# Opening of a two-block diffusion transformer kernel: first modulation tasks as rows on TensorE, token products in a first wave of four banks, token norm beside the QK products

## The reference

```python
def ada_chunks(cvec, w, b):
    m = jax.nn.silu(cvec) @ w + b
    return jnp.split(m[..., None, :], 6, axis=-1)

def modulate(x, g, shift, scale):
    return rms_norm(x, g) * (1 + scale) + shift

def chunk_gmlp(u, v, w_s, b_s, g_v):
    u = jax.nn.gelu(u)
    v = layer_norm(jax.nn.gelu(v), g_v)
    v = v.reshape(bn, length // A_CHUNK, A_CHUNK, A_GROUPS, A_GDIM)
    s = jnp.einsum('gij,bnjgc->bnigc', w_s, v) + b_s.T[None, None, :, :, None]
    return u * s.reshape(bn, length, A_WIDTH)

# layer 0
sh_m, sc_m, ... = ada_chunks(c, w_ada[0], b_ada[0])          # and for c_ctx
xm, cm = modulate(h, g, sh_m, sc_m), modulate(hc, g, csh_m, csc_m)
u, va, q, k, vb = split(t @ w_in)                            # t = xm and cm
y_a, y_b = chunk_gmlp(u, va, ...), neighbourhood_attention(q, k, vb, ...)
```

## Time and profile before

| | us |
|---|---|
| median of 3 runs (4460.9 to 4467.37) | 4466.56 |
| profiled execution, its own time | 4457.49 |
| its span | 4455.7 |
| PE busy | 3872.9 (87%) |
| DVE busy | 2122.0 (48%) |
| ACT busy | 1449.3 (33%) |
| POOL busy | 1549.5 (35%) |

### The profile page before, as it was taken

How to read it: one execution, slowest core, us unless ns; L and a number is a source line. 1 busy time by engine, 2 the same in 40 slices (tenths; PEclk the granted TensorE clock), 3 DMA queues, 4 the chain that set the end, 5 groups by cost and what they waited for, 6 DMA issues and landing times. The chain is left out here.

```text
span 4455.7 us, 51504 instructions
## 1 busy us (share of the span) xinstructions
PE 3872.9 (87%) x18628; PEld 3016.8 (68%) x18628; DVE 2122.0 (48%) x3651; ACT 1449.3 (33%) x2237; POOL 1549.5 (35%) x756
## 2 busy tenths in 40 slices
PE   1697889999887789998998777899989988778999
PEld 0685668888665668876886633588868866436887
DVE  4765777543446586644454846322232232552222
ACT  1225242222235633333223254322232233443222
POOL 0122124444221036553543311255535433104554
PEclk9798889999998989999999887999999998779999
DMA  6161124442120026753663210133322222102322
GB/s 208 45 175 19 41 63 136 150 142 66 33 59 4 12 74 219 231 167 114 226 217 103 62 38 1 38 95 99 95 75 94 91 74 67 28 1 62 98 91 75
DMA packets 460067, 410.80 MB, mean 92 GB/s; under 512 B 30095, under 2 KB 405007, under 8 KB 459919
## 3 DMA queue, kind: packets, MB, share of 16 engines
q1 hardware_dynamic: 447840, 400.53, 29.0%
q10 hardware_dynamic: 12079, 8.33, 0.6%
HBM read 405.14 MB, written 7.60 MB: 93 GB/s over the span
## 5 line engine op out<-in xcount | busy, mean ns | idle before, releaser
L198 POOL TENSOR_TENSOR s_wlo<-s_raw,s_whi 128x1024 fp32r<-128x1024 f32 x490 | 1185.0, 2426 | 2265.3 <-ACT s_whi L190 2264.9
L212 PE MATMUL psum<-s_xhi,s_whi 128*128 128x512 f32 x3264 | 1240.2, 380 | 127.3 <-DVE s_xlo L439 69.5
L213 PE MATMUL psum<-s_xlo,s_whi 128*128 128x512 f32 x3264 | 1231.4, 377 | 0.0
L214 PE MATMUL psum<-s_xhi,s_wlo 128*128 128x512 f32 x3264 | 1226.7, 376 | 0.0
L190 ACT ACTIVATE s_whi<-s_raw 128x1024 fp32r<-128x1024 f32 x490 | 509.2, 1054 | 1839.6 <-PE psum L214 1811.7
L212 PEld LDWEIGHTS psum<-s_xhi,s_whi 128*128 128x128 f32 x3264 | 622.4, 191 | 256.7 <-issue 140.4
L213 PEld LDWEIGHTS psum<-s_xlo,s_whi 128*128 128x128 f32 x3264 | 622.0, 191 | 115.0 <-issue 4.6
L214 PEld LDWEIGHTS psum<-s_xhi,s_wlo 128*128 128x128 f32 x3264 | 620.5, 190 | 114.4
L212 PE MATMUL psum<-s_ahi,s_whi 128*128 128x512 f32 x1232 | 481.4, 391 | 32.3 <-POOL s_wlo L198 22.7
L213 PE MATMUL psum<-s_alo,s_whi 128*128 128x512 f32 x1232 | 472.9, 384 | 0.0
L214 PE MATMUL psum<-s_ahi,s_wlo 128*128 128x512 f32 x1232 | 472.5, 384 | 0.0
(11 more groups left out here) (223 smaller groups left out, 4323.7 us busy)
## 6 DMA issues: line engine op xcount, KB each, us to landing
s_ada_raw<-w_ada SPq DMA_DIRECT2D x224, 512.0 KB, 3.9
s_raw<-w_gu SPq DMA_DIRECT2D x176, 512.0 KB, 3.8
s_raw<-w_up SPq DMA_DIRECT2D x88, 512.0 KB, 4.7
s_raw<-w_dn SPq DMA_DIRECT2D x88, 512.0 KB, 3.5
s_raw<-w_down SPq DMA_DIRECT2D x44, 512.0 KB, 4.7
s_raw<-w_in SPq DMA_DIRECT2D x28, 512.0 KB, 3.8
s_raw<-w_in_ab SPq DMA_DIRECT2D x20, 512.0 KB, 5.6
s_area<-w_ada SPq DMA_DIRECT2D x16, 512.0 KB, 10.4
```

Source lines behind the costliest of these rows:

```text
L198: pool.tensor_tensor(K.wlo[:, c % HL, 0:a * b], K.raw[:, c % RAW, 0:a * b], K.whi[:, c % HL, 0:a * b].bitcast(F32), ALU.subtract).then_inc ...
L212: pe.matmul(out, lh, rh, start=first, stop=False)
L213: pe.matmul(out, lh, rl, start=False, stop=False)
L214: return pe.matmul(out, ll, rh, start=False, stop=last)
```

## The change

The first two tasks move from DVE to PE. The columns of c and c_ctx come with the column constants, ACT takes their Silu (16 columns), and each block of 128 rows of the untransposed weights (`w_first`, a new input with the first 2048 columns of w_ada) is streamed past the two columns of c and c_ctx: 32 products of 512 columns into two PSUM rows. ACT copies the two rows of each task to SBUF, and eight products with a 2 x 2 identity turn them into columns, to which DVE adds the bias. This goes together with the first norm in one phase, `FirstNorm`; the loads of x come first on SP's queue, then the weights in twelve places instead of six. The constants that are not needed at once are loaded by ACT's queue behind the squares, the table copy `rpb` by SP's queue behind the first six chunks. `Begun` comes behind `FirstNorm`.

In the va projection t = 0 and t = 2 of the first two products (four banks) go along k by k, behind the split of both chunks; t = 1 follows. `Gmlp` is divided: `GmlpNorm` (token norm) stands in front of `SiluRows` and the q and k projection, `GmlpMix` and `U` behind it, and vb is a projection of its own, with no modulation blocks beside it; the 24 blocks stand with q and k, three instead of two for each chunk.

```diff
-FIRST = 6
+FIRST = 12
 class Start(Phase):
     def sp(self, e):
         e.dma_start(K.cols[:, :], K.io["cols"]).then_inc(K.sem["cols_in"], 16)
+        e.dma_start(K.h[:, :, 0:TX], K.io["xT"]...).then_inc(K.sem["x_in"], 16)
+        e.dma_start(K.h[:, :, TX:T0], K.io["ctxT"]...).then_inc(K.sem["x_in"], 16)
     def act(self, e):
+        for dst, src in K.early:
+            e.dma_start(dst, src).then_inc(K.sem["early_in"], 16)
+        e.wait_ge(K.sem["cols_in"], 16)
+        e.activation(K.ada_sum[:, :], K.cols[:, COLS["c"]:COLS["c"] + 16], ACT.Silu).then_inc(K.sem["first_silu"], 1)
...
 class Begun(Phase):
+    def sp(self, e):
+        self.ahead(e)
+        e.dma_start(K.rpb_rows, K.io["rpb"]...).then_inc(K.sem["rpb_in"], 16)
     def act(self, e):
-        self.loaded(e)
         for c in range(HL):
             split_hi(self.K, e, c)
...
+class FirstNorm(Norm):
+    def sp(self, e):
+        for c in range(8 * len(self.tasks)):
+            if c >= FIRST:
+                e.wait_ge(self.sem["first_used"], c - FIRST + 1)
+            t, k = divmod(c, 8)
+            e.dma_start(K.ada_first[:, c % FIRST, :], K.io["w_first"][k * P:(k + 1) * P, t * D:(t + 1) * D]).then_inc(
+                K.sem[f"first_rows{c % FIRST}"], 16)
+    def pe(self, e):
+        super().pe(e)
+        e.wait_ge(K.sem["first_silu"], 1)
+        for c in range(8 * len(self.tasks)):
+            t, k = divmod(c, 8)
+            e.wait_ge(K.sem[f"first_rows{c % FIRST}"], 16 * (c // FIRST + 1))
+            for a in range(0, D, BANK):
+                ins = e.matmul(self.rows(t)[:, a:a + BANK], K.ada_sum[:, 2 * k:2 * k + 2],
+                               K.ada_first[:, c % FIRST, a:a + BANK], start=(k == 0), stop=(k == 7))
+            ins.then_inc(self.sem["first_used"], 1)
+        for t in range(len(self.tasks)):
+            e.wait_ge(self.sem["first_row"], t + 1)
+            for m in range(8):
+                ins = e.matmul(self.columns(t)[:, 2 * m:2 * m + 2], K.ada_raw[0:2, t, m * P:(m + 1) * P], K.ident[0:2, 0:2],
+                               start=True, stop=True)
+            ins.then_inc(self.sem["first_col"], 1)
+    def act(self, e):
+        self.squares(e, 0, K.h, self.h_there)
+        for dst, src in K.consts:
+            e.dma_start(dst, src).then_inc(K.sem["const_in"], 16)
+        for t in range(len(self.tasks)):
+            e.wait_ge(self.sem["first_used"], 8 * t + 8)
+            e.activation(K.ada_raw[0:2, t, :], self.rows(t), ACT.Copy).then_inc(self.sem["first_row"], 1)
+        self.high(e)
+    def dve(self, e):
+        e.wait_ge(K.sem["x_in"], 32)
+        self.rsqrt(e, 0)
+        (the bias is added to the columns of each task, then:)
+        for s in range(2):
+            self.gains(e, s)
+        self.low(e)
...
+    def first_wave(self, e):
+        own = self.products[0][2]
+        e.wait_ge(K.sem["w_lo"], own[-1] + 1)
+        for k in range(8):
+            self.x_wait(e, k)
+            for i in range(2):
+                for t in (0, 2):
+                    q = (self.products[i][1] + t) * P
+                    three(e, self.tok_out(i, t), (K.xhi[:, k, q:q + P], K.xlo[:, k, q:q + P]),
+                          (self.two(K.whi, own, k), self.two(K.wlo, own, k)), k == 0, k == 7)
...
-        K.rows = SiluRows(K, (0, 1), start=True)
-        AdaOnly(K, mods[0:EARLY])
+        FirstNorm(K, T0, [(ng(0, 0), L0X, L0X + 8), (ng(0, 0), L0C, L0C + 8)], mods[0:EARLY])
         Begun(K)
         Load(K, [(K.pos_i, io["pos"].to_broadcast([P, TX]))])
-        Norm(K, T0, None, [(ng(0, 0), L0X, L0X + 8), (ng(0, 0), L0C, L0C + 8)])
         proj(T0, w_in, [... va ...], x_ready)
         BiasTable(K, [0], first_table)
-        Gmlp(K)
-        U(K, w_in)
         BiasKeep(K, [0], first_table)
+        GmlpNorm(K)
+        K.rows = SiluRows(K, (0, 1))
         jobs = [... q, k ...]
-        jobs += [(2048 + g * 256, 256, True, tokens_to(K.vtok, g * 256)) for g in range(2)]
-        K.rows = SiluRows(K, (0, 1))
         proj(T0, w_in, jobs, tasks=mods[EARLY:5])
+        GmlpMix(K)
+        U(K, w_in)
+        proj(T0, w_in, [(2048 + g * 256, 256, True, tokens_to(K.vtok, g * 256)) for g in range(2)])
         Split(K, [K.sT[:, g, :] for g in range(4)], T0, "ya_done")
```

More of the change, by code:

```diff
@@ L255, in sp @@
         K = self.K
-        if not self.start:
-            self.ahead(e)
-            e.wait_ge(self.sem["bias_ready"], self.at("bias_ready"))
+        self.ahead(e)
+        e.wait_ge(self.sem["bias_ready"], self.at("bias_ready"))
         for v, c in enumerate(self.vectors):
@@ L271, in row @@
             return self.K.pf[:, 6 * BANK:8 * BANK]
[L272 removed]
+        return self.K.ada_acc[:, 1, :]
     def dve(self, e):
@@ L278, with counts @@
 class Begun(Phase):
+    def counts(self):
+        return {"const_in": 16 * len(self.K.consts), "rpb_in": 16}
     def loaded(self, e):
-        e.wait_ge(self.K.sem["const_in"], 16 * (len(self.K.consts) + 2))
+        e.wait_ge(self.K.sem["const_in"], 16 * len(self.K.consts))
+    def sp(self, e):
+        K = self.K
+        self.ahead(e)
+        e.dma_start(K.rpb_rows, K.io["rpb"].unsqueeze(1).to_broadcast([120, GRID, P])).then_inc(K.sem["rpb_in"], 16)
     def act(self, e):
-        self.loaded(e)
         for c in range(HL):
@@ L360, in finish @@
         ins.then_inc(K.sem["ada_read"], 1)
[L363 to L380, removed]
 def newton(ph, e, total, r, tmp, T, i, n=1):
@@ L539, in dve, with __init__, counts, rows @@
             self.low(e)
+class FirstNorm(Norm):
+    def __init__(self, K, T, pre, tasks):
+        self.tasks = tasks
+        super().__init__(K, T, None, pre)
+    def counts(self):
+        n = len(self.tasks)
+        c = super().counts()
+        c.update(first_used=8 * n, first_row=n, first_col=n)
+        return c
+    def sp(self, e):
+        K = self.K
+        for c in range(8 * len(self.tasks)):
[4 more added lines that the diff above has]
+                K.sem[f"first_rows{c % FIRST}"], 16)
+    def rows(self, t):
+        return self.K.pf[0:2, (2 + 2 * t) * BANK:(4 + 2 * t) * BANK]
+    def columns(self, t):
+        return self.K.pf[:, (6 + t) * BANK:(6 + t) * BANK + 16]
+    def pe(self, e):
+        K = self.K
+        super().pe(e)
[13 more added lines that the diff above has]
+            ins.then_inc(self.sem["first_col"], 1)
+    def h_there(self, act, k):
+        act.wait_ge(self.K.sem["x_in"], 32)
+    def act(self, e):
+        K = self.K
+        self.squares(e, 0, K.h, self.h_there)
[6 more added lines that the diff above has]
+    def dve(self, e):
+        K = self.K
+        e.wait_ge(K.sem["x_in"], 32)
+        self.rsqrt(e, 0)
+        for t, dst in enumerate(self.tasks):
+            e.wait_ge(self.sem["first_col"], t + 1)
+            b = COLS["b_ada"] + 8 * t
+            for v in range(2):
+                ins = e.tensor_tensor(K.mod[:, dst[v]:dst[v] + 8], self.columns(t)[:, v::2], K.cols[:, b:b + 8], ALU.add)
+            ins.then_inc(K.sem["dve_step"], 1)
+            e.wait_ge(K.sem["dve_step"], K.step())
+        for s in range(2):
+            self.gains(e, s)
+        self.low(e)
@@ L699, in pe @@
                     ins.then_inc(self.sem["out_ready"], 1)
+        early = 2 if self.x_wait and self.products[0][1] is not None and T == T0 else 0
+        for i in range(early):
+            self.take(e, T, i)
+        if early:
+            self.first_wave(e)
         for i, ((_, n, _, _), tok, own) in list(enumerate(self.products))[pair:]:
-            self.take(e, T, i)
+            if i >= early:
+                self.take(e, T, i)
             if tok is None:
@@ L711, in pe @@
                 e.wait_ge(K.sem["w_lo"], own[-1] + 1)
-                for t in range(self.half):
-                    out = self.slot(T, i)[:, t * 2 * P:(t + 1) * 2 * P].rearrange("p (j c) -> p j c", j=2)
+                for t in range(self.half) if i >= early else (1,):
+                    out = self.tok_out(i, t)
                     for k in range(8):
-                        if i == 0 and t == 0 and self.x_wait:
+                        if i == 0 and t == 0 and not early and self.x_wait:
                             self.x_wait(e, k)
@@ L1063, in dve, with act, counts @@
         ins.then_inc(self.sem["v_ready"], 1)
+    def act(self, e):
+        K = self.K
+        e.wait_ge(self.sem["var_ready"], self.at("var_ready", 1))
+        e.activation(K.bag[:, :, 1], K.bag[:, :, 1], ACT.Sqrt, bias=K.eps[:, 0:1]).then_inc(self.sem["std_ready"], 1)
+class GmlpMix(Phase):
+    def counts(self):
+        return self.ring_counts(T0, 4)
+    def dve(self, e):
+        K = self.K
+        nt = T0 // P
         for g in range(4):
@@ L1071, in dve @@
             ins.then_inc(self.free(T0, g), 1)
[L1073 to L1076, removed]
     def pe(self, e):
         K = self.K
-        e.wait_ge(self.sem["v_ready"], self.at("v_ready", 1))
+        e.wait_ge(K.sem["const_in"], 16 * len(K.consts))
+        e.wait_ge(self.sem["v_ready"], self.at("v_ready"))
```

(2 more changed lines are left out.)

68 lines of the change are left out of this document (31 added, 37 removed).

## The result

The changed kernel took 4422.56 us (median of four runs, 4422.33 to 4424.0), the kernel before, on the same chip, 4466.19 (4460.9 to 4467.37): a ratio of 0.9905 with a 95% interval of 0.9888 to 0.9922, 43.6 us less. A repeat in another session gave 4425.69 against 4462.7, 0.9918 (0.9905 to 0.9932), 37.0 less. The forecast was 4438: the sign was right, and the change is worth 8 to 14 us more than the 29.2 of the sum.

A forecast was written before the change was run, and what follows sets the result against it. Bound: the opening's waits, modulation before the first norm, then the first projections' chain. 48.2 gained less 19.0 is 29.2: profiled 4457.5 to 4428.3, 4437.4 at the median, forecast 4438; own range 4427 to 4452, with rivals 4426 to 4470.

The forecast's parts named there:

- the 29.2 of the sum: Whole change: 48.2 us gained at the start of the norm's products, less 19.0 us of longer road behind it.
- N: Start of the first norm's products (L430) in the opening: forecast 60.2 us in place of 108.4, 48.2 gained.
- the rows, 32 products: PE, first norm: 32 products of 512 columns past two columns take 27.5 us, up to 32.
- the turn into columns: PE, behind the rows: 32 recorded small matmuls at the mix's 0.158 us each, 5.1 us; 2.0 by the skill.
- products 1, 3 read: First projection's token products: product 1 read at +42.7, 8.1 us later than before, product 3 at +67.6.
- wait at the mix: PE before the fourth mix group waits 24 us for DVE's 24 modulation blocks, where the removed stall comes back.
- half-clock rival: PE gets 1.2 GHz past two columns: rows end at 80, net gain 2.6 us, 4464 us; chance 0.35.
- With small waits: PE, q and k: eight products of 8.40 us come at once, done at +137 with only small waits.
- in time by a few us: SP's queue: nine blocks stand before the load of the seventh q/k chunk, which still comes in time.
- the table at +9: Range term for the bias table on DVE, taken from -4 to +9 us; seven POOL splits beside it priced at 4.
- Slower or faster blocks: Rivals on DVE's modulation blocks before the mix: slower, 4483 us, chance 0.08; faster, 64 us for 79.4, 4422 us, chance 0.07.
- the wave of four banks hides nothing: First projection: overlapping k with four banks gains nothing, as all of x is there when PE starts at +23.5.

The follow-up runs named there:

- the second profile: The kernel before, unchanged, profiled again: span 4463.6 us, one run 4465.36 us.
- the first profile: The kernel before, unchanged, in the profile the forecast rests on: span 4455.7 us, profiled execution 4457.5 us.
- the old order: The changed kernel with Gmlp and U in front of q and k again, vb back in their projection: 4410.08 us, 0.9882 of the kernel before.
- the kernel with two tasks: The changed kernel with two later modulation tasks (16 blocks) beside q and k, the third (8 blocks) beside vb: 4397.58 us, 0.9858 of the kernel before.

## Why the prediction was right in the opening and short in the sum

| from N, us | forecast | measured |
|---|---|---|
| N itself | 60.2 | 60.0 |
| x squared from | 14 | 14.3 |
| the rows, 32 products | 27.5 | 27.6 |
| the turn into columns | 5.1 | 3.7 |
| PE's first product | +23.5 | +23.0 |
| products 1, 3 read | +42.7, +67.6 | +42.7, +66.8 |
| last q/k product read | +137 | +158.9 |
| end of the modulation blocks | +166.7 | +168.8 |
| wait at the mix | 24 | 21.7 |
| last U read | +208.3 | +210.8 |
| end of the opening | +252.5 | +254.7 |

**The rows.** A column costs the same past 2 columns as past 128, 1.69 ns (27.63 over 32 x 512) against 1.68, and the granted clock stays at 1.00, 2.4 GHz. The half-clock rival, at 0.35 the largest, fell: two columns did not count as little. On transposes the run says nothing, and the 2 us that it took off for the time before the clock falls are shown by no run. The turn came out at 0.117 us for each recorded matmul (3.73 over 32), where the mix had 0.158. By an estimate from the 62 ns of the Trainium skill (TensorE: Matmul & The Clock Gate, Back-to-back issue gap) the turn would have been 2.0; the trace has 3.7, between that estimate and the row taken. That N agrees to 0.2 is in part luck: PE began the squares at 15.27, so they ended 1.0 late (28.03 for 27), and the turn was 1.4 shorter.

**The reads of q and k.** "With small waits" was wrong. I had SP's queue "in time by a few us" for the seventh chunk. It was not: ACT stood 22.2 us for it, with the read of the fourth product behind its split (178.18). Behind it three blocks stand in front of each chunk, and ACT's split in front of a read. This moved the stall from DVE to ACT and cost nothing of the sum, since DVE's blocks set the end by either way.

**The step that failed** is this sentence: "Behind that point both kernels run the same instructions in the same order, so the change is worth the move of that one time." PE's wait for the positions was removed at both places. In the opening that changed nothing of my sum, as the wait put back there costs nothing; but of the 51.5 us by which N comes earlier than in the second profile, 17.5 are to be had by dropping it alone, and I had put all of it down to the rows. At the output projection it was not priced at all: the waits of PE there are 6.0 to 6.4 us with it and 1.5 without. The distance between the two landmarks sums it up over all profiles:

| us between the landmarks | |
|---|---|
| with PE's wait | 216.8 and 214.9 (kernel before), 214.1, 217.5 |
| without it | 206.5 and 206.8 (changed kernel), 211.4, 210.8, 210.7, 210.6, 210.1, 210.1 |

No profile without the wait is as long as the shortest with it. The means, 215.8 and 209.6, differ by 6.2, but not all of that is the wait: without the changed kernel's two profiles the second mean is 210.6. From ACT's last read of the attention (L1313, L1401) to its first read of the output projection it is 26.4 to 27.5 us in the four profiles with PE's wait and 20.3 to 22.4 in the eight without it; in the pair compared above 26.5 and 22.3. So of the 8.4 us some 4 are the wait. The other 4 lie in the attention in front of it, and the largest part of them in its first 20 us. The windows there, first in the second profile of the kernel before, then in the changed kernel:

```profile
366.92:386.92 20.00, 14.47 (x71) 9.87 (x73) 12.34 (x36) 10.70 (x20) 0.96 (x1) 0.59 0.04 8
```

```profile
335.39:355.39 20.00, 14.47 (x104) 10.33 (x104) 13.99 (x40) 13.10 (x25) 0.95 (x1) 0.79 0.14 28
```

PE's granted clock was 0.59 and 0.79 over them, and within them the changed kernel draws 2.7 us ahead: ACT's fifth read of the attention starts 13.15 behind the landmark, not 15.89. Only the two profiles of the changed kernel have this, 0.79 and 0.78; the ten others have 0.59 to 0.61, with PE's wait or without. The prediction gave the attention nothing, and what brings the clock up earlier there stays open.

**The base.** The 29.2 was worked out on a profile whose opening was 4.3 quicker than that of the second profile, and then taken from the median. So against a profile nearer to the median, 42.9 = 31.5 in the opening + 8.4 to the second landmark + 3.0 in all that is behind it. Against the first profile the spans differ by 35.0. How large the typical opening is, two profiles can't settle, nor do the timed pairs fix the size of the `Load` edit beside the other changes closer than between nothing and some 10 us: their medians say 2 to 5, the spans 9 and 10. So the cause of the missed 8 to 14 us is shown in part only: the wait at the output projection for some 4 of them, in the traces. The clock in the attention and the base, for the rest, are argued from two profiles of each kernel. The upper end of the forecast's own range was also added up too low: with x at 23, the rows at 32, the turn at 6 and the table at +9 it is 4461, not 4452; the measured time lies below the lower end.

**The other rivals.** Slower or faster blocks: 24 blocks ended 2.1 later than forecast, so neither. That the wave of four banks hides nothing, as was forecast, agrees with product 1 read at +42.7.

## What to carry to other kernels

Before you say that two kernels are alike behind a point, go through every line of the diff, the waits in base classes and shared helpers above all, and look for each wait that it takes from an engine's queue in the chain of waits. What such a wait is worth depends on what else ends the stretch. Taken out alone, this one gave 20.6 us; beside the redesign, which moves the load out of its way, it is worth 0 to 10, and at the second layer's output projection next to nothing, as DVE's table ends that stretch. The gains of two edits that remove the same wait don't add. When work is moved under other work, count what then stands in front of it in the queue of the engine that reads it: moving eight blocks behind the mix turned a loss of some 14 us into a gain of some 12 against the old order.

## What the runs showed that was not expected

- A plain float32 product of 512 columns past a stationary of two columns took 0.43 us for each of its two recorded parts (27.63 over 64), and the granted clock was 1.00 over all 27.6 us, beside DMA traffic of 265 GB/s (30 to 55 us).
- A VectorE instruction beside a POOL split took some 2 us longer. The timeline of DVE in the kernel with two tasks, beside a split that began near 130:

```profile
129.35 0.43 DVE L1804 TENSOR_SCALAR s_t<-s_t 128x512 f32<-128x512 f32 x1
129.82 0.75 DVE L1807 SCALAR_TENSOR_TENSOR s_area<-s_t,s_small,s_area 128x512 f32<-128x512 f32 x1
130.60 2.51 DVE L1804 TENSOR_SCALAR s_t<-s_t 128x512 f32<-128x512 f32 x1
```

  The same instruction takes 0.43 and 2.51. Three more splits beside the table made it 6.5 longer, where 4 was allowed.
- Two profiles of the kernel before differ by 7.9 us in the span and by 3.1 already at N; a sum made on one of them carries that. Two of the changed kernel differ by 0.1 in the span.
